# Up product of three groups of eight by seven block products, with weight sums made by accumulating loads

## The chip, the cores and the metric

One core of one Trainium2 chip runs the whole computation as one program. The metric is the device time of one execution in microseconds (us). TensorE (PE) multiplies, VectorE (DVE), ScalarE (ACT) and GpSimd (POOL) do elementwise work, SyncE (SP) starts loads. The engines run side by side; each takes its own instructions in order and waits on semaphores.

## The reference

```python
def sqrelu_mlp(h, w1, w2):                      # w1 (1024, 4096), w2 (4096, 1024)
    u = jax.nn.relu(jnp.einsum('bsd,df->bsf', h, w1))
    return jnp.einsum('bsf,fd->bsd', u * u, w2)

for i in range(2):                              # h is (1, 512, 1024), float32
    hn = rmsnorm(h, norm_mix[i])
    h = h + (conformer_conv(hn, ...) if i == 0 else pool_mixer(hn, ...))
    h = h + sqrelu_mlp(rmsnorm(h, norm_mlp[i]), mlp_w1[i], mlp_w2[i])
return rmsnorm(h, final_norm)
```

The change concerns `sqrelu_mlp`, the dense part of both layers.

## The kernel before, in words

Every float32 operand is split into a high part, rounded to the multiplier's format, and a low part, the rest. A product is three matmuls: high x high, high x low, low x high (`product`, L1449; its matmuls are L1452 to L1454, those of the block products L1715 to L1717). For every weight or activation, ACT writes the high part (a copy) and DVE the low part (a subtraction).

The 4096 hidden features are cut into 8 groups of 512. A group has an up product and a down product. The up product (`mlp_up`, L1683) makes 4 tiles of 128 features x 512 tokens, each from 8 pieces of depth 128: 4 x 8 x 3 = 96 matmuls of 512 columns. For group 1 it is done in two halves of 256 tokens (`mlp_up_first`, L1720). Then ACT takes relu and square. The down product of groups 1 to 7 (`mlp_middle`, L1693) treats the group's product as 2 x 2 blocks and makes it by seven block products instead of eight (Strassen's scheme in Winograd's form): 7 x 12 = 84 matmuls of 512 columns. It needs sums of activation blocks (`a_sum`, DVE, 512 elements per partition) and sums of weight blocks (`b_sum_of`, DVE, 1024 elements). Two of the seven products stay in PSUM banks 4 to 7 over all groups; the other five go through banks 0 to 3, from which DVE adds them to `acc` or `h` (`add`, L1181). Group 8 is done directly (`mlp_up_last`, `mlp_down`).

The order on each engine is written out by hand. PE alternates up and down of a group without a break in the order. On DVE a group is one list: the low parts of the down weights (`b_low`) and of the next group's up weights (`w1_low`), the low parts of the activation blocks (`a_low`), the sums, and the adds. ACT has the matching list of high parts. SP loads the next group's weights whenever their raw copies have been read: up weights 2 MB at once (`load_m1`, L279), down weights in two halves of 1 MB (`load_m2`, L284). POOL has no work in the dense part, apart from clearing `acc`; earlier, in the convolution, it issues seven accumulating transfers within on-chip memory (L417, 1 MB each).

PE waits, for each piece, on semaphores that count finished low parts (`w1_lo_ok`, `w2_lo_ok`, `u_lo_ok`) and finished adds (`m_added`, since the banks are reused). In a block product these are the two lines

```python
pe.wait_ge(u_lo_ok, 7 * w + (LAYER_SPLITS * layer + i + 1))
pe.wait_ge(w2_lo_ok, 7 * w + (LAYER_SPLITS * layer + i + 1))
```

Of the kernel before, what the change touches and what calls it, by code (L numbers as in the profile page):

```python
# [23 lines left out]
P = 128  # L24
# [30 lines left out]
LAYER_ADDS = NQ + 10 * MIDDLE  # L55
LAYER_SPLITS = GF + 7 * MIDDLE
LAYER_SUMS = 4 * MIDDLE
UP_BANK = (2, 3, 0, 1)
# [5 lines left out]
def hybrid_encoder(nc, x, norm_mix, norm_mlp, conv_w1, conv_b1, conv_dw, conv_dwb, conv_ln_g, conv_ln_b,  # L64
                   conv_w2, conv_b2, pool_w, pool_b, pool_scale, mlp_w1, mlp_w2, final_norm, out):
    ctx = ExitStack()
    with ctx:
# [24 lines left out]
        spare = relu[:].rearrange("p a b -> p (a b)")  # L92
        tok = sb("tok", [P, 2, D])
        gain = sb("gain", [P, 2, D])
        ident = sb("ident", [P, P])

        with ExitStack() as share:
            params = share.enter_context(nc.sbuf_tensor("params", [P, NC, NPAR], F32))
        with ExitStack() as share:
            junk = share.enter_context(nc.sbuf_tensor("junk", [P, D], BF16))  # L100
# [3 lines left out]
        bn = sb("bn", [P, NB, 3, 6])  # L104
# [6 lines left out]

# [6 lines left out]
        with ExitStack() as share:  # L118
# [21 lines left out]
        b11, b12 = m2_raw[:, 0:2, 0:512], m2_raw[:, 0:2, 512:1024]  # L140
        b21, b22 = m2_raw[:, 2:4, 0:512], m2_raw[:, 2:4, 512:1024]
        t1, t2, t3, t4 = b_sum[:, 0], b_sum[:, 1], b12, b21
        a_parts = (a11, s3, a12, a22, s1, s2, s4)
        b_parts = (b11, t3, b21, t4, t1, t2, b22)
# [3 lines left out]
        qb_lo = w2_lo[:].rearrange("p (k f d) -> p k f d", k=4, f=2)  # L148
        c2_hi = (w1_hi[:].rearrange("p (c d) -> p c d", c=NC), w2_hi[:].rearrange("p (c d) -> p c d", c=NC))
# [52 lines left out]
        a_sum_ok, b_sum_ok, acc_zero, banks_read = (  # L202
            sem(n) for n in ("a_sum_ok", "b_sum_ok", "acc_zero", "banks_read"))

        w1_hi_ok, w1_lo_ok, w2_hi_ok, w2_lo_ok = (sem(n) for n in ("w1_hi_ok", "w1_lo_ok", "w2_hi_ok", "w2_lo_ok"))
# [55 lines left out]

        block = ctx.enter_context(nc.Block())
# [3 lines left out]
        def _(sp):  # L266
# [21 lines left out]

            def load_groups(layer):

                sp.wait_ge(w1_lo_ok, 4 * GROUPS * layer + 4)
                load_m1(layer, 1)

                def middle(w, more):
                    parts = LAYER_SPLITS * layer
                    sp.wait_ge(w2_lo_ok, 7 * w + (parts + 2))
                    load_m2(layer, w + 1, 0)
                    sp.wait_ge(w2_lo_ok, 7 * w + (parts + 7))
                    load_m2(layer, w + 1, 1)
                    if more:  # L300
                        sp.wait_ge(w1_lo_ok, 4 * w + (4 * GROUPS * layer + 8))
                        load_m1(layer, w + 2)

                with sp.Fori(0, MIDDLE - 1) as w:
                    middle(w, True)
                middle(MIDDLE - 1, False)
                sp.wait_ge(u_lo_ok, LAYER_SPLITS * layer + (LAYER_SPLITS - GF))
# [32 lines left out]
            for k in range(2):  # L340
                load_m2(0, 0, k)
# [6 lines left out]
            sp.dma_start(gain[:, 1, :], row(pool_scale[0])).then_inc(gain_in[1], 16)  # L348
            sp.wait_ge(turned, 4 * GEN_MLP0 + NB)
            sp.dma_start(pw_raw, pool_w[0].rearrange("g (k p) d -> p (g k) d", p=P)).then_inc(pw_in, 16)  # L350
            load_groups(0)
            sp.dma_start(gain[:, 0, :], row(norm_mix[1])).then_inc(gain_in[0], 16)
            sp.wait_ge(w1_lo_ok, 4 * GROUPS)
# [5 lines left out]
            for k in range(2):  # L359
                load_m2(1, 0, k)  # L360
            sp.wait_ge(tok_ok, 4 * GEN_POOL + NB)
            sp.dma_start(gain[:, 0, :], row(norm_mlp[1])).then_inc(gain_in[0], 16)
            load_groups(1)
# [122 lines left out]
        def _(act):  # L486
# [169 lines left out]
            def w1_high(layer, g, j):  # L656
                if j == 0:
                    act.wait_ge(w1_in, 16 * g + (32, 16 * (GROUPS + 2))[layer])
                nc.scalar.copy(m1_hi[:, j], m1_raw[:, j]).then_inc(w1_hi_ok, 1)  # L659
# [1206 lines left out]
```

## Time and profile before

| | |
|---|---|
| median of 3 runs | 886.23 us (885.8 to 886.63) |
| span of the profiled execution | 884.7 us |
| PE busy | 874.4 us, 99% of the span |
| DVE busy | 700.1 us, 79% |
| ACT busy | 464.1 us, 52% |
| POOL busy | 140.0 us, 16% |
| chain that ended last | PE 95%, DVE 2% |

The span is what the profile covers; no time of its own is given for the profiled execution, and the runs' median is 1.5 us over the span. A matmul is pipelined: its row shows 0.39 us, but the next starts 0.23 us later, so the cost of a matmul in a stream is the distance between starts. The same holds in part for DVE and ACT: two independent instructions in a row overlap a little.

### The profile page before, as it was taken

To read this page: it belongs to the slowest core of one execution; us is meant where nothing else is said; L and a number is where in the kernel's file an instruction comes from. 1 tells how busy PE (TensorE), PEld (TensorE's weight loads), DVE (VectorE), ACT (ScalarE), POOL (GpSimd) and SP (SyncE) were. 2 spreads that over 40 slices of the span, in tenths; PEclk is the share of its full clock that TensorE was granted. 3 is DMA by queue.
4 is the path that set the end of the run, shared out by engine and by line. 5 is a ranking of instruction groups with operands and counts; after the bars stand their busy time and mean duration, and the time that the engine had idled before them with its cause. 6 is when DMAs were issued, how large, how long until landed. Compare 5 with 4: busy or idle time off the path is not lost.

```text
span 884.7 us, 11889 instructions
## 1 busy us (share of the span) xinstructions
PE 874.4 (99%) x4383; PEld 740.7 (84%) x4383; DVE 700.1 (79%) x946; ACT 464.1 (52%) x675; POOL 140.0 (16%) x122
## 2 busy tenths in 40 slices
PE   8999999999999999999999999999999999999997
PEld 8888887899888888888888889988888888888886
DVE  6899999768786968776778788897786968776866
ACT  6898976247272544536273544637272544536243
POOL 1699970560000020000000040000000000000000
PEclk9999999999999999999999999999999999999999
DMA  9766732305413142331314222122313142331202
GB/s 302 198 166 150 188 73 98 143 1 191 143 47 143 57 175 77 118 133 57 142 48 167 77 73 90 48 98 94 142 47 142 52 174 77 125 127 64 72 1 95
DMA packets 49255, 97.62 MB, mean 110 GB/s; under 512 B 1562, under 2 KB 18978, under 8 KB 48324
## 3 DMA queue, kind: packets, MB, share of 16 engines
q1 hardware_dynamic: 48068, 89.54, 29.4%
q0 software_dynamic: 1008, 7.34, 4.0%
q8 instruction: 23, 0.38, 0.2%
q10 hardware_dynamic: 144, 0.26, 0.1%
q14 instruction: 12, 0.10, 0.0%
HBM read 87.70 MB, written 2.10 MB: 101 GB/s over the span
## 4 chain that ended last, share of the span: by engine, by line
PE 95%; DVE 2%; DMA 1%; ACT 1%; issue 0%; SPq 0%; DVEq 0%; ACTq 0%
PE ps L1454 19%; PE ps L1452 19%; PE ps L1453 19%; PE ps L1717 10%; PE ps L1715 10%; PE ps L1716 10%; PE ps L1530 3%; PE ps L1471 1%; PE ps L1629 1%; PE ps L1634 1%; PE ps L1630 1%; DMA h<-in_x 1%; DVE tok L894 0%; DVE act_lo L900 0%; DVE tok L928 0%
## 5 line engine op out<-in xcount | busy, mean ns | idle before, releaser
L1452 PE MATMUL ps<-act_hi,w_hi 128*128 128x512 f32 (+1 forms) x688 | 254.9, 370 | 0.0
L1453 PE MATMUL ps<-act_lo,w_hi 128*128 128x512 f32 (+1 forms) x688 | 254.2, 369 | 0.0
L1454 PE MATMUL ps<-act_hi,w_lo 128*128 128x512 f32 (+1 forms) x688 | 254.2, 369 | 0.0
L1715 PE MATMUL ps<-w_hi,u_hi 128*128 128x512 f32 x392 | 152.7, 390 | 0.0
L1717 PE MATMUL ps<-w_hi,u_lo 128*128 128x512 f32 x392 | 152.7, 390 | 0.0
L1716 PE MATMUL ps<-w_lo,u_hi 128*128 128x512 f32 x392 | 152.5, 389 | 0.0
L685 ACT ACTIVATE relu<-ps 128x512 f32<-128x512 f32 x36 | 21.5, 597 | 242.8 <-PE ps L1454 242.8
L1452 PEld LDWEIGHTS ps<-act_hi,w_hi 128*128 128x128 f32 x688 | 129.7, 188 | 21.8
L1454 PEld LDWEIGHTS ps<-act_hi,w_lo 128*128 128x128 f32 x688 | 129.6, 188 | 21.8
L1453 PEld LDWEIGHTS ps<-act_lo,w_hi 128*128 128x128 f32 x688 | 129.7, 188 | 21.7
L1172 DVE TENSOR_TENSOR w_lo<-w_raw,w_hi 128x1024 fp32r<-128x1024 f32 x70 | 85.1, 1220 | 58.0 <-ACT w_hi L706 58.0
L1118 DVE TENSOR_TENSOR w_lo<-w_raw,w_hi 128x1024 fp32r<-128x1024 f32 x64 | 76.9, 1223 | 12.4 <-ACT w_hi L659 12.4
L1717 PEld LDWEIGHTS ps<-w_hi,u_lo 128*128 128x128 f32 x392 | 73.6, 188 | 15.6
L1716 PEld LDWEIGHTS ps<-w_lo,u_hi 128*128 128x128 f32 x392 | 73.6, 188 | 15.4
L1715 PEld LDWEIGHTS ps<-w_hi,u_hi 128*128 128x128 f32 x392 | 73.6, 188 | 15.2
L706 ACT CAST w_hi<-w_raw 128x1024 fp32r<-128x1024 f32 x70 | 73.0, 1046 | 19.6 <-PE ps L1717 13.3
L1183 DVE TENSOR_TENSOR h<-h,ps 128x512 f32<-128x512 f32 x84 | 57.2, 681 | 31.7 <-PE ps L1717 31.7
L991 DVE SCALAR_TENSOR_TENSOR ps<-upad,params,ps 128x512 f32<-128x512 f32 x107 | 71.2, 748 | 0.0
L659 ACT CAST w_hi<-w_raw 128x1024 fp32r<-128x1024 f32 x64 | 66.3, 1044 | 6.6 <-DMA w_raw<-in_mlp_w 6.6
L560 ACT ACTIVATE prod_a<-upad,params 128x512 f32<-128x512 f32 x64 | 40.4, 712 | 2.6 <-DMA prod_a<-prod_a 2.6
L1183 DVE TENSOR_TENSOR acc<-acc,ps 128x512 f32<-128x512 f32 x56 | 37.0, 680 | 3.4 <-PE ps L1717 3.4
L1172 DVE TENSOR_TENSOR w_lo<-b_sum,w_hi 128x1024 fp32r<-128x1024 f32 x28 | 34.1, 1218 | 0.5 <-ACT w_hi L706 0.5
(237 smaller groups left out, 1264.0 us busy)
## 6 DMA issues: line engine op xcount, KB each, us to landing
w_raw<-in_mlp_w SPq DMA_DIRECT2D x32, 1024.0 KB, 5.0
w_raw<-in_mlp_w SPq DMA_DIRECT2D x16, 2048.0 KB, 8.0
w_raw<-in_conv_w SPq DMA_DIRECT2D x16, 512.0 KB, 5.5
prod_a<-prod_a POOLq DMA_DIRECT2D x7, 1024.0 KB, 7.9
w_raw<-in_conv_w SPq DMA_DIRECT2D x2, 2048.0 KB, 11.0
h<-in_x SPq DMA_DIRECT2D x4, 512.0 KB, 5.8
out<-tok SPq DMA_DIRECT2D x7, 256.0 KB, 2.0
gain<-in_norm_mlp SPq DMA_DIRECT2D x2, 512.0 KB
```

Of the source, the lines that this page charges most:

```text
L659: nc.scalar.copy(m1_hi[:, j], m1_raw[:, j]).then_inc(w1_hi_ok, 1)
L706: nc.scalar.copy(qb_hi[:, i % 4], b_parts[i]).then_inc(w2_hi_ok, 1)
L991: step = nc.vector.scalar_tensor_tensor(into, window, weight, sums[n % 2], ALU.mult, ALU.add)
L1118: nc.vector.tensor_tensor(m1_lo[:, j], m1_raw[:, j], m1_hi[:, j].bitcast(F32), ALU.subtract).then_inc(w1_lo_ok, 1)
L1172: nc.vector.tensor_tensor(qb_lo[:, i % 4], b_parts[i], qb_hi[:, i % 4].bitcast(F32), ALU.subtract).then_inc(w2_lo_ok, 1)
L1183: nc.vector.tensor_tensor(at, at, ps[:, k % 4, :], op).then_inc(m_added, 1)
L1452: nc.tensor.matmul(dst, lh, rh, start=(n == 0), stop=False)
L1453: nc.tensor.matmul(dst, lh, rl, start=False, stop=False)
L1454: return nc.tensor.matmul(dst, ll, rh, start=False, stop=(n == count - 1))
L1715: nc.tensor.matmul(dst, lh, rh, start=(f == 0 and (opens or i not in (0, 5))), stop=False)
L1716: nc.tensor.matmul(dst, lh, rl, start=False, stop=False)
L1717: last = nc.tensor.matmul(dst, ll, rh, start=False, stop=(f == 1 and (closes or i not in (0, 5))))
```

## The change

Groups 2 to 7 of a layer go in pairs. In the first of a pair ("plain", groups 2, 4, 6) the up product stays as it was. In the second ("blocks", groups 3, 5, 7) it is made by seven block products too. Written `w` from 0, group 1 is w = 0, and pair v is w = 2v+1 and 2v+2. The parts of the change:

- PE: a block product of the up side is 2 feature tiles x 4 depth pieces x 3 = 24 matmuls of 256 columns; seven of them make 168.
- Activations: four block sums of the activations (z1 to z4) are made once a layer, on DVE in group 1 (`x_block`, `x_step`, eight instructions), and split (`x_high`, `x_low`).
- Results: the seven products are put together by seven DVE instructions (`sum_two` ... `sum_21`) before relu and square, and one ACT copy.
- Weight sums: the up weights of a blocks group come as four loads of 512 KB. Of the sums, two are made by DVE or are plain blocks; the others grow in one buffer (`w_chain`) by accumulating loads that POOL issues (`add_s1`, `add_s2`, `add_s4`), each after its forerunner has been split. The down weights come as four loads of 512 KB as well; two of the four DVE sums per group become accumulating loads (`add_t2`, `add_t4`).
- Down product: the order of the seven products changes (banks 4 to 7 take the first and the fourth), and each pair of adds of 512 elements becomes one of 1024.
- The load of the pool weights in layer 0 moves behind the last blocks group's up product; the POOL descriptor scratch is set to 4096 bytes.

The core of the diff:

```diff
-LAYER_ADDS = NQ + 10 * MIDDLE
+LAYER_ADDS = NQ + 5 * MIDDLE
+W_AT = (1, 3, 4, 2, 5, 7, 6)
+B_AT = (1, 3, 2, 4, 5, 6, 7)
...
+            def w_source(layer, g, upper_f, upper_k):
+            return (mlp_w1[layer].rearrange("(c p) f -> p c f", p=P)
+                    [:, 4 * upper_k:4 * upper_k + 4, bass.ds(g * 512 + 256 * upper_f, 256)])
...
+            def add_w(layer, g, into, upper_f, upper_k, done):
+                nc.gpsimd.dma_start(into, w_source(layer, g, upper_f, upper_k), accum_op=ALU.add).then_inc(done, 16)
+            def add_s2(layer, v):
+                pool.wait_ge(acc_zero, layer + 1)
+                pool.wait_ge(w1_lo_ok, block_part(layer, v) + W_AT[1])
+                add_w(layer, 2 * v + 2, w_chain, 0, 0, w_chain_added)
...
+                with pool.Fori(0, PAIRS) as v:
+                    add_t2(layer, 2 * v + 1)
+                    add_s1(layer, v)
+                    add_t4(layer, 2 * v + 1)
+                    add_s2(layer, v)
+                    add_s4(layer, v)
+                    add_t2(layer, 2 * v + 2)
+                    add_t4(layer, 2 * v + 2)
...
 # ACT, third and fourth up tile of a plain group, and the late parts
+                    up_tile(n + 2, done + 3, banks[2], squared[1][:, 0], lambda: chain_b(3, 1))
+                    up_tile(n + 3, done + 4, banks[3], squared[1][:, 1])
+                    act.wait_ge(usq_ok, n + 4)
+                    sums_high()
...
 # DVE, group 1 ("first") and plain groups
+                    b_low(0)
+                    if kind == "plain":
+                        w1_low(plain_part(layer, v) + 2, 2)
+                    b_sum_three()
+                    b_sum_one()
+                    if kind == "plain":
+                        w1_low(plain_part(layer, v) + 3, 3)
                     b_low(2)
+                    b_low(1)
+                    if kind == "first":
+                        x_block(layer, 1, z1, 1, 1)
+                        x_block(layer, 2, z3, 0, 1)
+                        x_step(layer, 3, z3, z1, z3, ALU.subtract)
+                        x_block(layer, 4, z2, 0, 0)
+                        x_step(layer, 5, z2, z3, z2, ALU.add)
+                        x_step(layer, 6, z1, z1, z2, ALU.subtract)
+                    third_sum(n + 2)
                     a_low(0)
                     a_low(1)
+                    if kind == "plain":
+                        w_low(layer, v, 0)
+                    b_low(3)
+                    first_sum()
+                    second_sum()
+                    a_low(2)
+                    a_low(3)
+                fourth_sum()
+                if kind == "plain":
+                    w_low(layer, v, 3)
+                b_low(4)
+                add(1, 0, acc[:, 1])
+                a_low(4)
+                if kind == "plain":
+                    w_low(layer, v, 1)
+                add(2, 2, acc[:, 0])
+                b_low(5)
                 a_low(5)
                 b_low(6)
                 a_low(6)
+                add(4, 4, h[:, 0:2, 0:512])
+                if kind == "plain":
+                    w_low(layer, v, 2)
+                    w_sum_three()
+                add(5, 6, h[:, 2:4, 0:512])
+                add(6, 8, h[:, 0:2, 512:D])
+                if kind == "first":
+                    x_low(layer, 0)
+                    x_block(layer, 7, z4, 1, 0)
+                    x_step(layer, 8, z4, z4, z2, ALU.subtract)
+                    x_low(layer, 1)
+                    x_low(layer, 2)
+                    x_low(layer, 3)
...
 # PE, up product of a blocks group
+                for i, bank in enumerate((2, 3, 0, 1, 0, 1, 2)):
+                    pe.wait_ge(w1_lo_ok, n + W_AT[i])
+                    if i < 4:
+                        pe.wait_ge(m_added, 5 * w + (LAYER_ADDS * layer - 1 + i // 2))
...
+                    for j in range(2):
+                        for c in range(4):
+                            nc.tensor.matmul(dst, lh, rh[:, c], start=(c == 0), stop=False)
+                            nc.tensor.matmul(dst, lh, rl[:, c], start=False, stop=False)
+                            last = nc.tensor.matmul(dst, ll, rh[:, c], start=False, stop=(c == 3))
```

## Rows read from the trace of the kernel before

**Rows 1.** The page: busy time by engine, and the granted clock in 40 slices.

```profile
PE 874.4 (99%) x4383; PEld 740.7 (84%) x4383; DVE 700.1 (79%) x946; ACT 464.1 (52%) x675; POOL 140.0 (16%) x122
PEclk9999999999999999999999999999999999999999
```

**Rows 2.** Windows (length; PE, PEld, DVE, ACT, POOL busy; clock; DMA; GB/s): group 3, up, down.

```profile
272.86:294.64 21.78, 21.78 (x98) 18.03 (x97) 15.43 (x15) 11.11 (x15) 0.00 (x0) 1.00 0.31 109
294.64:313.70 19.06, 19.06 (x85) 15.76 (x84) 15.06 (x21) 8.04 (x11) 3.95 (x2) 1.00 0.26 98
```

**Rows 3.** Windows, one middle group of 40.80 us.

```profile
336.10:376.90 40.80, 40.80 (x181) 33.73 (x181) 30.49 (x36) 19.09 (x27) 0.00 (x0) 1.00 0.29 103
```

**Rows 4.** Timeline of DVE in a middle group's down product.

```profile
340.41 0.68 DVE L1167 TENSOR_TENSOR u_lo<-relu,u_hi 128x512 fp32r<-128x512 f32 x1
341.01 1.22 DVE L1172 TENSOR_TENSOR w_lo<-b_sum,w_hi 128x1024 fp32r<-128x1024 f32 x1
342.15 0.68 DVE L1183 TENSOR_TENSOR acc<-acc,ps 128x512 f32<-128x512 f32 x1
342.75 0.68 DVE L1176 TENSOR_TENSOR a_diff<-gain,relu 128x512 f32<-128x512 f32 x1
```

**Rows 5.** Timeline of DVE, group 1 of layer 0, up to its first down product.

```profile
200.92 1.22 DVE L1179 TENSOR_TENSOR b_sum<-w_raw 128x1024 f32<-128x1024 f32 x1
202.24 1.23 DVE L1179 TENSOR_TENSOR w_raw<-w_raw 128x1024 f32<-128x1024 f32 x1
204.51 3.49 DVE L1172 TENSOR_TENSOR w_lo<-w_raw,w_hi 128x1024 fp32r<-128x1024 f32 x3
208.66 0.69 DVE L1176 TENSOR_TENSOR a_diff<-relu 128x512 f32<-128x512 f32 x1 [0.65 <-ACT relu L689]
209.31 0.69 DVE L1167 TENSOR_TENSOR u_lo<-relu,u_hi 128x512 fp32r<-128x512 f32 x1
```

**Rows 6.** Timeline of ACT after the first up tile of a group.

```profile
319.36 0.60 ACT L685 ACTIVATE relu<-ps 128x512 f32<-128x512 f32 x1 [14.76 <-PE ps L1454]
319.86 1.04 ACT L706 CAST w_hi<-w_raw 128x1024 fp32r<-128x1024 f32 x1
320.79 0.63 ACT L689 ACTIVATE relu<-relu 128x512 f32<-128x512 f32 x1
```

**Rows 7.** Timeline of PE, matmuls of 256 columns, 188.15 to 190.91 (24 in all).

```profile
188.15 0.28 PE L1452 MATMUL ps<-act_hi,w_hi 128*128 128x256 f32 x1
...
190.91 0.28 PE L1454 MATMUL ps<-act_hi,w_lo 128*128 128x256 f32 x1
```

**Rows 8.** Timeline of PE: the first down matmul of layer 0.

```profile
212.92 0.39 PE L1715 MATMUL ps<-w_hi,u_hi 128*128 128x512 f32 x1
```

**Rows 9.** The line of POOL's accumulating transfers, seven of 1 MB.

```profile
L417 POOL DMA_DIRECT2D prod_a<-prod_a x7: 855/863/1044, 37.7 to 115.9; - x7
DMA to landing us min/median/max: 6.9/7.9/12.3
```

**Rows 10.** DMA view of 115 to 124 us, one such transfer alone.

```profile
q0 software_dynamic: 144, 1.05, 57.7%
prod_a<-prod_a POOLq DMA_DIRECT2D x1, 1024.0 KB, 6.9
```

**Rows 11.** DMA view of 60 to 75 us: packets of two kinds.

```profile
q1 hardware_dynamic: 2735, 1.38, 34.7%
q0 software_dynamic: 144, 1.05, 33.7%
```

**Rows 12.** DMA view of 306 to 325 us: the weight loads of a group.

```profile
w_raw<-in_mlp_w SPq DMA_DIRECT2D x1, 2048.0 KB, 7.9
```

More of the change, by code:

```diff
@@ L294, in middle @@
[L294 to L305, printed above, removed]
@@ new lines, in load_groups @@
+                sp.wait_ge(w1_lo_ok, LAYER_PARTS * layer + GF)
+                load_m1(layer, 1)
+                load_first(0)
+                load_rest(0)
+                with sp.Fori(0, PAIRS - 1) as v:
+                    pair(v)
+                pair(PAIRS - 1, closes=True)
+                if layer == 0:
+                    sp.wait_ge(up_mm, block_part(0, PAIRS - 1) + PARTS)
+                    sp.dma_start(gain[:, 1, :], row(pool_scale[0])).then_inc(gain_in[1], 16)
+                    sp.dma_start(pw_raw, pool_w[0].rearrange("g (k p) d -> p (g k) d", p=P)).then_inc(pw_in, 16)
@@ L830, in _ @@
             act_high(GEN_MLP1, 3)
-            mlp_middle(1, 0, True)
-            with act.Fori(1, MIDDLE) as w:
-                mlp_middle(1, w)
+            mlp_middle(1, 0, "first")
+            with act.Fori(0, PAIRS) as v:
+                mlp_middle(1, v, "plain")
+                mlp_middle(1, v, "blocks")
             mlp_up_last(1)
@@ L1156, in mlp_add, with mlp_middle @@
                 nc.vector.tensor_tensor(at, at, mlp_bank(q), ALU.add).then_inc(m_added, 1)
-            def mlp_middle(layer, w, first=False):
+            def mlp_middle(layer, v, kind):
+                w = {"first": 0, "plain": 2 * v + 1, "blocks": 2 * v + 2}[kind]
                 splits = LAYER_SPLITS * layer
@@ L1206, in mlp_middle, with second_sum, fourth_sum @@
+                def second_sum():
+                    dve.wait_ge(u_lo_ok, 7 * w + (splits + 1))
+                    a_sum(2, s2, s1, a11, ALU.subtract)
+                def fourth_sum():
+                    dve.wait_ge(usq_ok, n + 4)
+                    dve.wait_ge(u_lo_ok, 7 * w + (splits + 2))
+                    a_sum(3, s4, a12, s2, ALU.add)
+                if kind == "blocks":
                     b_low(0)
+                    b_sum_three()
+                    b_sum_one()
+                    w_low(layer, v, 4)
+                    b_low(2)
@@ L1240, in mlp_middle @@
-                dve.wait_ge(a_sum_ok, 4 * w + (sums + 3))
-                dve.wait_ge(u_lo_ok, 7 * w + (splits + 2))
-                a_sum(s4, a12, s2, ALU.subtract)
-                add(2, 0, 2, h_tile(0, 0))
+                    first_sum()
+                    second_sum()
+                    a_low(2)
+                    a_low(3)
+                fourth_sum()
+                if kind == "plain":
+                    w_low(layer, v, 3)
+                b_low(4)
+                add(1, 0, acc[:, 1])
@@ L1244, in mlp_middle @@
+                a_low(4)
+                if kind == "plain":
+                    w_low(layer, v, 1)
+                elif kind == "blocks":
+                    w1_low(plain_part(layer, v + 1), 0)
+                else:
+                    w1_low(plain_part(layer, 0), 0)
+                add(2, 2, acc[:, 0])
+                b_low(5)
                 a_low(5)
-                add(2, 1, 3, h_tile(1, 0))
-                b_low(5)
-                add(3, 0, 4, h_tile(2, 0), ALU.subtract)
                 b_low(6)
@@ L1381, in _ @@
             act_low(GEN_MLP1, 3)
-            mlp_middle(1, 0, True)
-            with dve.Fori(1, MIDDLE) as w:
-                mlp_middle(1, w)
+            mlp_middle(1, 0, "first")
+            with dve.Fori(0, PAIRS) as v:
+                mlp_middle(1, v, "plain")
+                mlp_middle(1, v, "blocks")
             mlp_up_last(1, lambda j: merge(1, j))
```

601 lines of the change are left out of this document (419 added, 182 removed).

## The prediction

> **What bounds the kernel now.** I read the page first: PE is busy for 99% of the span at full granted clock [rows 1], so only fewer or shorter matmuls, or a PE that waits, can move the time. Then windows on one middle group: 96 up matmuls take 21.78 us and 84 down matmuls 19.06 us, 0.227 us each, the group 40.84 us, with no gap [rows 2]. The same group keeps DVE busy for 30.5 us and ACT for 19.1 us [rows 3]. So PE is the bound, and DVE has 10 us to spare in a group; but its list is in fixed order, so the question is whether single results come in time for PE, more than whether the sum fits. Last the timelines, for the distance from start to start: on DVE 0.60 us after an instruction of 512 elements and 1.14 after one of 1024, 1.22 where the next needs its result [rows 4]; up to 1.32 in a dependent pair [rows 5]. On ACT 0.50 and 0.95 [rows 6].
>
> **The matmuls.** A blocks group replaces 96 matmuls of 512 columns (21.78 us) by 168 of 256. In the stream of narrow ones, 24 starts span 2.76 us, 0.120 each [rows 7]. 168 x 0.120 = 20.16 us, so a blocks group saves 1.62 us, and three in each of two layers save 9.7 us. That is all the change can give; the work on other engines gives nothing back while PE is the bound.
>
> Half of 0.227 would be 0.1135, and 16 us; the row says that a narrow matmul costs more than half a wide one. The Trainium skill (TensorE: Matmul & The Clock Gate, Back-to-back issue gap) gives N / 2.4 + 2.5 ns for an isolated stream: 216 ns for 512 columns and 109 for 256, by which the saving would be an estimated 14.5 us. The rows show 227 and 120, both 11 ns over it, and 11 ns on 168 matmuls instead of 96 is what the saving loses.
>
> **Group 1: the activation sums.** Before, DVE begins the group's list at 200.92, the low part that the first block product needs is done at 209.31 + 0.69 = 210.0, and PE begins the down product at 212.92: 2.9 us of slack [rows 5, 8]. The change takes out one of three weight sums ahead of it (-1.14 us net; the ACT handshakes around the two that are left give some of it back, since the high part of b_low(2) can only start when the second sum is done) and puts six sums of 1024 elements in, each waiting for the last: 6 x 1.22 = 7.3 us [rows 4]. The slack of 2.9 becomes a wait of 7.3 - 1.1 - 2.9 = 3.3, and I take 3.4 for the handshake. Nothing covers it: PE has nothing else queued, it stands in the wait for `u_lo_ok`. The bounds: 2.9 (1.14 each) to 3.9 us (1.32 each) [rows 5]. Both layers: 6.8 us.
>
> **The chain of accumulating loads.** All depends on L, the time from POOL's issue to the landing of 512 KB. Row: an accumulating 1 MB alone lands after 6.9 us, median 7.9, 12.3 at worst beside other loads [rows 9, 10]. In the window of 9 us its packets take 57.7%, 5.2 us, so about 1.8 us are fixed. Half the bytes: 1.8 + 2.6 = 4.4 us, the lower end. But those pieces were 8 KB; an up-weight piece is now 1 KB, eight times as many, and comes from HBM. Loads of 512-byte pieces took 34.7% of 15 us x 16 engines for 2735 packets, 0.03 us each [rows 11], so the fixed part of a piece is below 0.03, and 28 more pieces per engine cost at most 0.8 us. POOL's own 0.86 us for writing 128 pieces would be 3.4 for 512 if it grew in proportion: +2.6. Upper end 4.4 + 0.8 + 2.6 = 7.8, and to 9 if other loads are beside it. I take L = 5.5, nearer to the row of the transfer alone.
>
> The Trainium skill (DMA: Bandwidth & Descriptors, Anatomy of one DMA) gives about 2.0 us + bytes / 436e3 for a load issued by POOL: an estimated 3.2 us here, 4.4 for 1 MB. The row of 6.9 for 1 MB speaks against it for accumulating transfers; by it the waits of the next paragraphs would nearly vanish and the time be that of the first rival.
>
> In a plain group, from the start T of the down product: ACT's relu and square of the last tile end at T + 1.4; DVE then has s1, s2, a_low(2), a_low(3), s4 (3.2 us with their waits), w_low(3), b_low(4), add(1) (3 x 1.14), a_low(4) 0.60 and w_low(1) 1.22: T + 9.9. There POOL issues s2. When it has landed, ACT's high part (1.04), w_low(2) (1.14), the sum s3 (1.14) and add(5) (1.22) follow, since add(5) is queued behind them on DVE: T + 9.9 + L + 4.5. PE wants bank 2, which add(5) frees, for the up product of the blocks group at T + 19.06. So PE waits L - 4.65 us: 0.87 at L = 5.5. Before, the adds stood at the end of the list behind nothing that a transfer could hold. The second and third pair of a layer pay this: 1.7 us per layer.
>
> **The first pair is worse.** After its adds of group 1, DVE still has six instructions for the activation blocks, 7.0 us. They move group 2's list: counted from the start of the up product, add(6) ends at 1.3, those six at 8.3, the five before b_low(2) at 14.0, b_low(2) at 15.2 instead of 8.2, and only then may POOL issue t2. ACT waits for t2 between the relu of the third tile and its square, and relu of the fourth tile stands behind. It shares the DMA engines with the 2 MB of the blocks group, issued at the same time and 7.9 us on their way [rows 12], so I give it L + 2.6 = 8.1 us: 15.3 + 8.1 + 0.95 + 0.5 + 0.6 = 25.4, and PE needs that relu at 21.8 + 2.7 = 24.5. Wait 0.9. From there a_low(5) is 11.3 us of DVE list away and PE's fifth block product 4 x 2.72 = 10.9 plus the start of the list, which leaves 1.0, and 0.2 for an add. The s2 chain then starts 0.7 later against PE than in the other pairs: 0.87 + 0.7 = 1.6. Together 3.7 us per layer (0.7 at L = 4.4; 7.8 at L = 7.4).
>
> **Edits that cost nothing.** The 1024-element adds instead of two of 512 (1.14 for 1.20) [rows 4]; the seven sums after the up product of a blocks group: small DVE instructions, 18 per group against 11, in a group with 39.2 us of PE and, by counting its list (19 x 1.14 + 18 x 0.60), 32.5 us of DVE. The copy and sums between block product seven and down product two have 2.7 us of the first down product over them: three dependent steps of 0.68, relu 0.60 included where it counts. If that cover were gone it would cost 1 to 2 us per blocks group. s1, s4, t4 and the sixth down part have 8 us or more from issue to use, so they show from L = 8 on. The moved pool weights have the up product of group 8 over them (21.8 us against 6 for loading and 4.8 for scaling on POOL).
>
> **The sum.** Per layer 3.4 + 3.7 + 1.7 = 8.8 us of waits, less 4.9 saved: +3.9. Two layers: +7.8 us, on a span of 884.7 and 1.5 around it, the median of 886.2: **894.0 us**. Slower.
>
> **Rivals.**
> - *The accumulating loads hide* (the other side: not slower). One mechanism: s2 lands within 4.65 us of its issue, so add(5) is never late. The lower end of 4.4 is for it, the smaller pieces against. (The 3.2 us of the Trainium skill's DMA: Bandwidth & Descriptors would be for it too.) Then a layer waits 3.4 + 0.7 and saves 4.9: 886.2 - 1.6 = 884.6. It decides at about L = 4.7, where waits equal the saving.
> - *They are long.* L = 7.4, as by POOL writing four times the pieces: 3.4 + 7.8 + 2 x 2.7 = 16.6 per layer, less 4.9, twice: +23.4, 909.6. For it, the 12.3 us beside other loads [rows 9]; against it, that s2 runs nearly alone.
> - *Narrow matmuls at half price*, or DVE's list in group 1 less late than counted, with loads hidden: 16.3 or 9.7 saved against 8 or 2 of waits, 878 in both. Against it, the even distance of 0.120 in this very mix of operands [rows 7].
> - *PE's queues don't block as read*, and the change costs nothing net though the loads are as forecast: within 1.5 us of 886.
>
> **Chances.** Forecast (L from 4.9 to 6.6, 888.5 to 902) 0.52; long 0.20; hidden loads 0.14; cheap matmuls or no hold in group 1 0.09; no net effect 0.05. The range 884.4 to 906 leaves out the cheap case and the long tail. Two tenths of a percent, 1.8 us, is what can be told from no change here: faster (below 884.4) 0.11, within 0.15, slower 0.74.
>
> **What would show it.** The first down matmul of each layer's group 1 with an idle of about 3.4 us, released by DVE's low part. Idle of 1 us ahead of the up product of groups 5 and 7, released by an add, and more ahead of group 3. Accumulating loads of 512 KB landing in 5 to 6 us. The narrow matmuls 0.120 apart. I am wrong if PE stays at 99% busy, or if idle PE time lies inside the blocks groups, where I have none.

## The result, and the profile after

The changed kernel takes 927.08 us (median, 925.02 to 928.47); the kernel before, on the same chip, 886.49 (885.8 to 886.89). The ratio is 1.0457, with a 95% interval of 1.0444 to 1.0470: slower by 4.6%. The forecast was 894.0 with a range up to 906. The direction was right; the extra time is five times what I gave it (40.6 us instead of 7.8).

The page of the kernel after, in the parts that answer to [rows 1]:

```profile
span 926.8 us, 13179 instructions
PE 880.6 (95%) x4815; PEld 762.2 (82%) x4815; DVE 751.7 (81%) x938; ACT 498.3 (54%) x707; POOL 197.9 (21%) x168
PE   8999999998988999999898999899899989999997
PEclk9999999999999999999998999999999999999999
q0 software_dynamic: 18128, 31.46, 20.4%
PE 57%; DVE 26%; DMA 8%; issue 5%; ACT 3%; DVEq 0%; SPq 0%; POOLq 0%; ACTq 0%
```

PE went from 99% busy to 95%, and a quarter of the chain that ended last is now DVE's. What PE waited for (engine and line that waits, what released it, us in total, times, longest):

```profile
PE ps L2063 <- DVE h L1492: 17.5, 6, 4.1
PE ps L2097 <- DVE u_lo L1464: 12.9, 5, 3.8
PE ps L2097 <- ACT gain L841: 4.9, 2, 3.4
PE ps L1832 <- POOL ident L501: 1.7, 1, 1.7
```

The fourth line was there before; the other three are new, 35.3 us in thirteen waits. L2063 is the first matmul of a blocks group's up product, which waits for add(5) to free its bank; L2097 is a down matmul behind an activation's low part, or behind ACT's relu of the group's last up tile. Counted as distance from start to start beyond 0.227 or 0.120 us, the same thirteen gaps are 37.5 us.

That explains 37.5 - 9.7 = 27.8 us of the 42.1 by which the span grew (884.7 to 926.8). The rest doesn't show as waiting. PE's timeline behind the first of the gaps, in group 1 of layer 0:

```profile
216.90 0.79 PE L2097 MATMUL ps<-w_hi,u_hi 128*128 128x512 f32 x1 [3.61 <-DVE u_lo L1464]
217.49 0.63 PE L2098 MATMUL ps<-w_lo,u_hi 128*128 128x512 f32 x1
217.92 0.63 PE L2099 MATMUL ps<-w_hi,u_lo 128*128 128x512 f32 x1
...
219.62 0.54 PE L2097 MATMUL ps<-w_hi,u_hi 128*128 128x512 f32 x1
220.01 0.39 PE L2098 MATMUL ps<-w_lo,u_hi 128*128 128x512 f32 x1
```

The starts are 0.43 us apart, not 0.227: half the clock, 1.2 GHz instead of 2.4, for seven matmuls, which cost 220.01 - 216.90 - 7 x 0.227 = 1.5 us more. The windows show it as granted clock (columns as in [rows 2]; the clock stands after the five busy times):

```profile
200.00:210.00 10.00, 10.00 (x85) 10.00 (x85) 8.85 (x8) 5.77 (x8) 1.27 (x1) 1.00 0.66 232
210.00:220.00 10.00, 6.39 (x35) 5.57 (x34) 8.59 (x9) 3.69 (x6) 0.11 (x1) 0.83 0.30 52
490.00:500.00 10.00, 6.19 (x17) 4.61 (x16) 8.43 (x7) 3.51 (x5) 3.80 (x2) 0.66 0.34 115
600.00:610.00 10.00, 10.00 (x33) 7.97 (x34) 7.99 (x10) 8.09 (x12) 1.21 (x1) 0.72 0.45 90
```

In the last of them PE is 100% busy and starts 33 matmuls of 512 columns in 10 us, where 44 would fit. Seven such stretches cost 13.0 us (1.5, 1.6, 1.5, 2.6, 2.8, 1.6, 1.5), longer distances of single matmuls 1.7. Each of the seven follows one of the ten gaps of 2.5 us or more; three of these ten (3.6, 3.0 and 2.9 us) and the three gaps below 2 us are followed by none. So: gaps 37.5, low clock 14.7, narrow matmuls -9.7, together +42.5, against a measured +42.1.

### The profile page after: what moved, and what is told of

Its sections match the earlier page's. It is cut to its first block, busy times and chain, and to the rows that moved or that the text cites. A ratio compares the mean times of both kernels' runs of the same rounds, so it can differ in the third digit from the quotient of the medians.

```text
span 926.8 us, 13179 instructions
## 1 busy us (share of the span) xinstructions
PE 880.6 (95%) x4815; PEld 762.2 (82%) x4815; DVE 751.7 (81%) x938; ACT 498.3 (54%) x707; POOL 197.9 (21%) x168
## 3 DMA queue, kind: packets, MB, share of 16 engines
q0 software_dynamic: 18128, 31.46, 20.4%
## 4 chain that ended last, share of the span: by engine, by line
PE 57%; DVE 26%; DMA 8%; issue 5%; ACT 3%; DVEq 0%; SPq 0%; POOLq 0%; ACTq 0%
PE ps L1799 8%; PE ps L1797 8%; PE ps L1798 8%; DVE ps L1236 7%; PE ps L2097 5%; PE ps L2098 5%; PE ps L2099 5%; PE ps L2063 5%; PE ps L2065 4%; PE ps L2064 4%; DMA w_raw<-in_mlp_w 4%; DMA b_sum<-in_mlp_w 3%; DVE w_lo L1469 2%; DVE w_lo L1390 1%; PE ps L1816 1%
## 5 line engine op out<-in xcount | busy, mean ns | idle before, releaser
L1797 PE MATMUL ps<-act_hi,w_hi 128*128 128x512 f32 (+1 forms) x496 | 180.5, 364 | 0.0
L1799 PE MATMUL ps<-act_hi,w_lo 128*128 128x512 f32 (+1 forms) x496 | 179.5, 362 | 0.0
L1798 PE MATMUL ps<-act_lo,w_hi 128*128 128x512 f32 (+1 forms) x496 | 179.5, 362 | 0.0
L2097 PE MATMUL ps<-w_hi,u_hi 128*128 128x512 f32 x392 | 156.8, 400 | 17.8 <-DVE u_lo L1464 12.9
L1797 PEld LDWEIGHTS ps<-act_hi,w_hi 128*128 128x128 f32 x496 | 93.7, 189 | 14.8 <-issue 0.3
L1799 PEld LDWEIGHTS ps<-act_hi,w_lo 128*128 128x128 f32 x496 | 93.6, 189 | 14.5
L2097 PEld LDWEIGHTS ps<-w_hi,u_hi 128*128 128x128 f32 x392 | 75.3, 192 | 36.7 <-DVE u_lo L1464 12.4
L2099 PEld LDWEIGHTS ps<-w_hi,u_lo 128*128 128x128 f32 x392 | 75.1, 192 | 16.2
L851 ACT CAST w_hi<-b_sum 128x1024 fp32r<-128x1024 f32 x42 | 43.9, 1046 | 69.8 <-DVE b_sum L1479 48.9
L869 ACT CAST w_hi<-w_raw 128x1024 fp32r<-128x1024 f32 x42 | 43.6, 1051 | 61.0 <-DMA w_raw<-in_mlp_w 46.8
L1390 DVE TENSOR_TENSOR w_lo<-w_raw,w_hi 128x1024 fp32r<-128x1024 f32 x42 | 50.8, 1222 | 27.9 <-ACT w_hi L869 27.9
L1469 DVE TENSOR_TENSOR w_lo<-w_raw,w_hi 128x1024 fp32r<-128x1024 f32 x56 | 68.3, 1220 | 0.0
L851 ACT CAST w_hi<-w_raw 128x1024 fp32r<-128x1024 f32 x56 | 58.7, 1048 | 17.6 <-PE ps L2099 17.6
L1492 DVE TENSOR_TENSOR h<-h,ps 128x1024 f32<-128x1024 f32 x42 | 50.7, 1219 | 18.5 <-PE ps L2099 18.3
L2063 PE MATMUL ps<-act_hi,w_hi 128*128 128x256 f32 x144 | 43.8, 304 | 17.5 <-DVE h L1492 17.5
## 6 DMA issues: line engine op xcount, KB each, us to landing
w_raw<-in_conv_w SPq DMA_DIRECT2D x2, 2048.0 KB, 10.7
```

The source lines that it names most:

```text
L851: nc.scalar.copy(qb_hi[:, i % 4], b_parts[i]).then_inc(w2_hi_ok, 1)
L1390: nc.vector.tensor_tensor(wp_lo[:, i % 4], w_parts[i], wp_hi[:, i % 4].bitcast(F32), ALU.subtract).then_inc(w1_lo_ok, 1)
L1469: nc.vector.tensor_tensor(qb_lo[:, i % 4], b_parts[i], qb_hi[:, i % 4].bitcast(F32), ALU.subtract).then_inc(w2_lo_ok, 1)
L1492: nc.vector.tensor_tensor(at, at, ps[:, k % 4:k % 4 + 2, :], ALU.add).then_inc(m_added, 1)
L1797: nc.tensor.matmul(dst, lh, rh, start=(n == 0), stop=False)
L1798: nc.tensor.matmul(dst, lh, rl, start=False, stop=False)
```

## The experiments

"The changed kernel" is the one of 927.08 us. The gaps of each run are counted from the PE timeline of its one profiled execution in the same way. "Slow matmuls" is what the half-clock stretches and the longer distances of single matmuls cost together, 14.7 us in the changed kernel. In the diffs "..." marks lines left out, and the arguments of `x_block` and `x_step` are left out too.

**The adds first.** In plain groups add(5) goes ahead of the wait for the low part of s2's sum:

```diff
+                if kind == "blocks":
+                    w1_low(plain_part(layer, v + 1) + 1, 1)
+                elif kind == "first":
+                    w1_low(plain_part(layer, 0) + 1, 1)
+                add(5, 6, h[:, 2:4, 0:512])
                 if kind == "plain":
                     w_low(layer, v, 2)
                     w_sum_three()
...
-                add(5, 6, h[:, 2:4, 0:512])
                 add(6, 8, h[:, 0:2, 512:D])
```

> In every plain group the add of banks 2 and 3 stands ahead of w_low(2) and w_sum_three on DVE, so it no longer waits for the accumulating load s2. Theory A (PE waits for that add because it is queued behind s2): the six idle stretches ahead of the up product of groups 3, 5 and 7 (4.22, 2.56, 3.04, 2.90, 2.95 and 2.80 us, 18.5 in all) go, and with them the four stretches of half clock behind them (1.60, 1.48, 1.56, 1.48: 6.1 us): 927 - 24.6 = about 902.5 us. Rival B (the load itself is late for PE): the idle time moves to the third up block product, which needs w_low(2), and the time stays above 915 us.

Measured 904.37 us, 1.0207 (1.0182 to 1.0233): 22.7 us less than the changed kernel, though only an add changed places with two instructions. The line "PE <- DVE h" is gone from its waits:

```profile
PE ps L2097 <- DVE u_lo L1464: 11.2, 3, 4.0
PE ps L2097 <- ACT gain L841: 5.4, 2, 3.1
```

The six gaps were 18.5 us; the slow matmuls shrank by 3.5 us (14.7 to 11.2) and the gaps that are left by 1.5, 23.5 in all against 23.4 between the two traced executions. This is close to what theory A said (902.5). It was the place of add(5) in DVE's queue that let a transfer hold PE, and nothing that PE itself needed from s2.

**The same loads without accumulation.** The POOL loads only overwrite; bytes, places and waits stay.

```diff
-, accum_op=ALU.add).then_inc(done, 16)
+).then_inc(done, 16)
```

> POOL's loads of the weight blocks don't accumulate (the weight sums are left out, the block is only overwritten); issue, size and waits are the same. Theory A (an accumulating load is slower than a plain one of the same pieces by the read and add on the chip's side): landing falls from 6.0 and 6.6 us to under 5, and the time to about 915 us. Rival B (what costs is the small pieces and POOL's writing of them): landing stays at 6 us and the time at 927.

Measured 903.12 us, 1.0191 (1.0172 to 1.0210), below both. Issue and landing, first of the changed kernel (instruction's duration in ns min/median/max, then issue to landing in us, for the loads of L581):

```profile
L581 POOL DMA_DIRECT2D w_raw<-in_mlp_w x18: 1264/1296/1316, 257.6 to 835.6; - x18
DMA to landing us min/median/max: 6.0/6.6/11.3
```

and without accumulation, with its queue's row (packets, MB, share of 16 engines):

```profile
q0 software_dynamic: 7632, 31.46, 11.9%
L581 POOL DMA_DIRECT2D w_raw<-in_mlp_w x18: 748/768/777, 258.5 to 812.4; - x18
DMA to landing us min/median/max: 4.1/4.3/8.3
```

The same 31.46 MB go in 7632 packets instead of 18128; POOL writes them in 0.77 us instead of 1.30, and they land 2.3 us sooner. The add gaps, 2.6 to 4.2 us each, fall to 0.58 to 0.84, all gaps together from 37.5 to 18.4 us and the slow matmuls from 14.7 to 8.6: 24 us less, twice the 12 of theory A. The pieces are the same in both, so rival B, small pieces and POOL's writing of them, is out as the main cost. The packets say what accumulation does. Seven 1 MB transfers take 7 x 144 = 1008 of either number [rows 10]. The 46 loads of the change have 6624 left without accumulation, 144 each; with it 17120, which is 18 x (512 + 16) + 28 x (256 + 16): one packet for every contiguous piece, of 1 KB in the 18 up-weight loads and of 2 KB in the 28 down-weight loads, where the plain load makes 144 of any. But the number of packets isn't the whole cost: beyond the plain load, 528 packets cost 2.3 us of landing time (6.6 against 4.3) and 272 cost 2.0 (6.0 against 4.0). What the rest goes into was not separated.

**Without the activation sums.** The eight sums and four splits per layer are left out, on ACT and DVE; the products take plain quarters. The part on PE:

```diff
-                        pe.wait_ge(x_lo_ok, X_PARTS * layer + right[i] + 1)
-                        rh, rl = x_hi[right[i]], x_lo[right[i]]
+                    cs, cols = act_quarter(*(right[i] if i in (0, 3, 5) else (i % 2, i // 4)))
+                    rh, rl = act_hi[:, cs, cols], act_lo[:, cs, cols]
```

> Leaves out the four activation block sums and their split; the blocks products read plain quarters of the activations in their place, so the number and size of matmuls is the same. Theory A (the sums on DVE hold group 1 and delay the list of group 2): the idle of 3.77 and 3.78 us in group 1 goes, with 1.5 and 2.8 us of half clock; group 2 keeps only what the other pairs have, so its three idle stretches of 8.96 and 5.61 us become about 2.8 each; 927 - 11.9 - 9.0 - 1.6 = about 904.5 us. Rival B (group 2 is late because its loads are slow, not because of the list): only the first part goes, 915 us.

Measured 909.31 us, 1.0249 (1.0231 to 1.0268): 17.8 us less. Group 1's gap falls from 3.8 to 1.4 and 0.9 us, and both gaps inside group 2 are gone, but its add gap stays (4.4 and 2.7). The miss of 5 us against theory A's 904.5 is what stays: in layer 0 the sums are not all of the first pair's extra wait (4.4 us against the 2.7 to 2.8 of the other pairs), and in group 1 a wait for ACT's relu takes the place of the sums, behind the split of the chained load:

```profile
PE ps L2074 <- ACT gain L841: 1.9, 2, 1.2
```

**The pool weights later.** The two SP loads go behind the last `load_m2` of the layer.

```diff
-                if layer == 0:
-                    sp.wait_ge(up_mm, block_part(0, PAIRS - 1) + PARTS)
-                    sp.dma_start(gain[:, 1, :], row(pool_scale[0])).then_inc(gain_in[1], 16)
-                    sp.dma_start(pw_raw, pool_w[0].rearrange("g (k p) d -> p (g k) d", p=P)).then_inc(pw_in, 16)
...
                 load_m2(layer, GROUPS - 1, 1)
+                if layer == 0:
+                    sp.wait_ge(up_mm, block_part(0, PAIRS - 1) + PARTS)
+                    sp.dma_start(gain[:, 1, :], row(pool_scale[0])).then_inc(gain_in[1], 16)
+                    sp.dma_start(pw_raw, pool_w[0].rearrange("g (k p) d -> p (g k) d", p=P)).then_inc(pw_in, 16)
```

> The two loads for the pooling layer (0.5 and 1 MB) are issued after the last down weights and not beside the accumulating load t4 of group 7 in layer 0. Theory A (t4, 10.66 us there against 6.0 in the median, is slow because of them, and POOL's multiplications, which start when they land, slow DVE): idle of 3.97 us and 2.6 us of half clock go, 920.5 us. Rival B (t4 is late for another reason): 927 us, and t4 still takes over 9 us.

Measured 919.83 us, 1.0376 (1.0359 to 1.0393), near theory A's 920.5: 7.3 us for a step that I had costed at nothing. In the changed kernel (timelines of POOL, SP, DVE and PE in group 7's down product of layer 0):

```profile
476.94 1.19 POOL L584 DMA_DIRECT2D b_sum<-in_mlp_w  x1 [11.31 <-DVE w_lo L1469]
488.10 5.70 POOL L631 TENSOR_TENSOR tok<-tok,gain 128x1024 f32<-128x1024 f32 x2 [9.98 <-DMA tok<-in_pool_w]
...
477.41 0.43 SPq L409 DMA_DIRECT2D tok<-in_pool_w  x1
...
488.71 2.88 DVE L1469 TENSOR_TENSOR w_lo<-b_sum,w_hi 128x1024 fp32r<-128x1024 f32 x1 [1.85 <-ACT w_hi L851]
491.51 2.84 DVE L1464 TENSOR_TENSOR u_lo<-gain,u_hi 128x512 fp32r<-128x512 f32 x1
494.28 1.21 DVE L1469 TENSOR_TENSOR w_lo<-w_raw,w_hi 128x1024 fp32r<-128x1024 f32 x1
...
494.41 0.80 PE L2097 MATMUL ps<-w_hi,u_hi 128*128 128x512 f32 x1 [3.81 <-DVE u_lo L1464]
```

Two things meet. POOL's chained load t4 and the pool weights are issued 0.5 us apart, and both take some 10.7 us until their user starts. Then POOL scales the pool weights, 2.85 us an instruction, and DVE's two instructions beside it take 2.88 and 2.84 us, where such ones take 1.22 and 0.69. The first of them waits for t4, and the second is what PE waits for. The Trainium skill (SBUF — State Buffer, Who interferes with whom) says that a DVE instruction with two SBUF inputs contends with a GpSimd instruction that reads SBUF; these rows agree, and show that even an instruction of half the length runs for as long as POOL's.

The late load alone would have cost PE next to nothing: by an estimate from these rows, with the usual 1.14 and 0.69 us the second one ends at 490.5, and PE has its matmul queued from 490.4. In the run without accumulation DVE doesn't wait for t4 at all, and the same two instructions beside POOL still take 3.17 and 2.84 us (gap 2.3). And it matters which instructions stand beside POOL. The kernel before had these two multiplications in the dense part as well (it is not so that POOL only cleared `acc` there), beside adds with one input in a PSUM bank, and neither side got slower, POOL at 2.4 us each and DVE at 0.64 (1.28 for two):

```profile
309.49 1.28 DVE L1183 TENSOR_TENSOR acc<-acc,ps 128x512 f32<-128x512 f32 x2
309.75 4.76 POOL L474 TENSOR_TENSOR tok<-tok,gain 128x1024 f32<-128x1024 f32 x2 [117.53 <-DVE w_lo L1118]
```

With the loads later it is so again (POOL 4.79 us for both at 498.60, DVE's adds beside them as fast as ever), and t4 lands after 5.3 us instead of 10.7.

The gap (4.0 us) and its half-clock stretch (2.6) are gone, 6.6 us, and the medians differ by 7.3. That the two agree so well is in part luck. The trace has eight half-clock stretches where the changed kernel's has seven, behind other gaps, and the gaps that both have are 3.5 us shorter, 2.7 of them in the first pair of layer 0 (6.3 us instead of 9.0), which runs ahead of the edit. A single traced execution gives such gaps to 1 to 3 us only.

**Both queue moves.** The adds first and the pool weights later.

> The add first and the pooling loads late; the activation sums stay in group 1. By the two kernels with one of these moves each (904.4 and 919.8 against 927.1): 904.4 - 7.3 = 897.1 us. Left are the two idle stretches of 3.77 us in group 1 with 1.5 to 2.9 us of half clock behind each, and those of group 2's relu, 2.5 to 3.3 us with 1.5. Rival B: the moves don't add up, because one covers part of the other, above 900 us.

Measured 897.82 us, 1.0125 (1.0111 to 1.0140). The two moves add: 22.7 + 7.3 = 30.0, and 29.3 are measured, as forecast (897.1). What is left is group 1 (gaps of 3.8 us) and the ACT relu of group 2 behind t2 (3.5 us), in each layer, and a gap of 1.1 us in group 2 of layer 1.

**Three moves.** The activation sums and splits leave group 1 as well. They are spread over group 2 and the start of group 3 (the last two splits, with `b_low(1)` behind one of them), and the first pair is taken out of the loop on ACT and DVE for it. Whether writing the pair out changes the time by itself was not tried.

```diff
+                early = isinstance(v, int) and v == 0 and kind != "first"
...
                     b_low(1)
-                    if kind == "first":
-                        x_block(1), x_block(2), x_step(3), x_block(4), x_step(5), x_step(6)
+                    if early and kind == "plain":
+                        x_block(1), x_block(2)
                     third_sum(n + 2)
...
                         w_low(layer, v, 0)
+                    if early and kind == "plain":
+                        x_step(3), x_block(4), x_step(5)
                     b_low(3)
+                    if early and kind == "plain":
+                        x_step(6), x_block(7), x_step(8)
...
+                if early and kind == "plain":
+                    x_low(layer, 0)
                 add(5, 6, h[:, 2:4, 0:512])
+                if early and kind == "plain":
+                    x_low(layer, 1)
```

> The add of banks 2 and 3 first, the pooling loads late, and the activation sums moved out of group 1: the eight sums stand in the up product of group 2, where DVE waits for relu and square, the four splits at its end and in group 3 (the first pair is written out of the loop for that). Theory A (every idle stretch comes from the order of the DVE list or from the pooling loads, and the saving of 9.7 us by narrow matmuls is real): idle of 2 to 4 us in all is left, no half clock, 879 us, faster than before the change. Rival B (the accumulating loads hold the list in other places as well): new idle ahead of the third up block product or in the down products, over 886 us.

Measured 885.55 us, 0.9995 (0.9986 to 1.0003): the time of before, not the 879 of the theory. Eight gaps of 0.6 to 1.6 us, 8.1 us in all, and some 2 us of longer distances of single matmuls use up the 9.7. There is no half clock: the windows of these groups show a granted clock of 1.00 (the next expectation calls 2.7 us half-clock stretches; they are single matmuls). All gaps are in groups 1 to 3. Rival B had a part in it, since the longest, 1.56 us in group 1, stands behind the chained load. In the later half of group 2 and the start of group 3 DVE now works without a pause, from 255.2 to 297.4 us. If that is the cause, each us taken out of this stretch comes out of the gaps; the next three runs try it.

**Three sums back into group 1.** The first three sums stand in group 1, behind the second activation split, and one split less in group 3.

```diff
+                    if kind == "first":
+                        x_block(1), x_block(2), x_step(3)
                     b_low(3)
...
-                        x_low(layer, 2)
                         b_low(1)
...
+                if early and kind == "plain":
+                    x_low(layer, 2)
                 add(6, 8, h[:, 0:2, 512:D])
```

> The version with all three moves, with its activation sums placed once more: the first three of the nine steps (3.4 us of VectorE) go into group 1, behind the second activation split, where VectorE of the trace of three moves idles 5.2 us (211.62 to 216.86) for the weight split behind the chained load; the other six stay in group 2, and the third of the four activation splits goes to the end of group 2 instead of into group 3's up product. The theory (a us of VectorE in a stretch where it is saturated is a us of TensorE, the same us in VectorE's idle time is free): the gaps of 1.10, 0.81 and 1.00 us (layer 0) and 1.10, 0.84 and 1.01 us (layer 1) in groups 2 and 3 go, 5.9 us together, the gap of 1.56 and 0.62 us behind the late chained load in group 1 stay, and the half-clock stretches (2.7 us) stay or shrink: 885.6 - 5.9 = 879.7, range 878 to 882.5. The rival (VectorE has no slack left in group 1 either, since TensorE waits there for whatever is put ahead of the fourth weight split): group 1's gap grows by up to 3.4 us per layer with its half-clock stretch, and the time is 885 to 890.

Measured 886.48 us, 1.0001 (0.9992 to 1.0010): a miss, by 6.8 us. Group 1 took the sums for next to nothing (in layer 0 its gap fell from 1.56 to 0.77, in layer 1 it grew from 0.3 to 0.7). But I had emptied 2.9 us of DVE's time at the start of group 2 and put nothing there, so that the later half of the group was as full as before. Of the gaps that were to go, those of group 2 stayed (0.97 and 1.13 us), and the two of group 3, 0.8 and 1.0, became one of 1.88 in each layer. Behind the one in layer 1 the clock fell to half, which cost 1.4 us.

**Sums into idle time.** The fourth and fifth sum go ahead of `third_sum` in group 2, the sixth ahead of `b_low(3)`.

```diff
                     b_low(1)
+                    if early and kind == "plain":
+                        x_block(4), x_step(5)
                     third_sum(n + 2)
```

> The version before it had three activation sums moved into group 1's idle time of VectorE, but left 2.9 us of VectorE idle at the start of group 2 (244.06 to 247.04, waiting for the relu of ScalarE) that the version of three moves had filled with two sums, and so was no faster (gap of 1.88 us behind a late sum in group 3, in both layers). Here the fourth and fifth steps (2.5 us) go into that idle time, and the sixth into the 1.5 us at 252.9 to 254.5; nothing else changes. The theory (a us counts only where VectorE is saturated from there to the next need of TensorE): VectorE enters the second half of group 2 about 3.4 us earlier than with three moves, the gaps of 0.97 and 1.13 us in group 2 and 1.88 us in group 3 of both layers go, with the half-clock stretches behind them (1.6 us in layer 1): 886.5 - 7.5 = 879.0, range 877.5 to 881.5. The rival (what binds in groups 2 and 3 is the landing of the chained loads or another chain, not VectorE's queue): the gaps move by less than 1 us, and the time is 885 to 888.

Measured 884.60 us, 0.9973 (0.9961 to 0.9984), 5.6 us over the forecast. The gaps in group 2 went (0.6 us are left in layer 1), and the half clock (none is left in this trace, in group 1 either, though the next expectation counts on some); those in group 3 stayed, and the gap of group 1 in layer 0 was back at 1.5, with no edit there. The trace says why group 3 gained nothing. DVE in group 2:

```profile
250.63 1.22 DVE L1393 TENSOR_TENSOR x_raw<-x_raw,tok 128x1024 f32<-128x1024 f32 x1
254.94 1.23 DVE L1469 TENSOR_TENSOR w_lo<-b_sum,w_hi 128x1024 fp32r<-128x1024 f32 x1 [3.09 <-ACT w_hi L851]
```

It idles 3.1 us for the split behind t2 and then does the last two sums, which wait for nothing there.

**The last two sums ahead of that wait.**

```diff
+                        x_block(7), x_step(8)
                     b_low(3)
-                    x_block(7), x_step(8)
```

> The version before it left VectorE idle for 3.09 us (251.8 to 254.94, layer 0) and 3.55 us (layer 1) in group 2, waiting for the weight split behind a chained load, and ran the last two activation sums (2.5 us) right behind that wait; the gap of 1.86 and 1.88 us in group 3 behind a late sum stayed. Here these two sums stand ahead of that wait; nothing else changes. The theory: VectorE is 2.5 us earlier from there on, both gaps of 1.9 us go, those of group 1 (1.5 us and its half-clock stretches) stay: 884.6 - 3.7 = 880.9, range 879.5 to 882.5. The rival (the sum in group 3 is late because of another chain, the loads of the blocks behind it): the time stays at 884 to 885.

Measured 882.90 us, 0.9960 (0.9947 to 0.9974). DVE there now:

```profile
249.65 1.22 DVE L1393 TENSOR_TENSOR x_raw<-x_raw,tok 128x1024 f32<-128x1024 f32 x1
250.90 1.23 DVE L1393 TENSOR_TENSOR gain<-act_hi,act_lo 128x1024 f32<-128x1024 f32 x1
252.16 1.23 DVE L1393 TENSOR_TENSOR gain<-gain,tok 128x1024 f32<-128x1024 f32 x1
253.47 1.23 DVE L1469 TENSOR_TENSOR w_lo<-b_sum,w_hi 128x1024 fp32r<-128x1024 f32 x1
256.74 0.69 DVE L1488 TENSOR_TENSOR relu<-relu,gain 128x512 f32<-128x512 f32 x1 [2.05 <-ACT gain L845]
```

It is faster than the kernel before by 0.4%, 3.6 us, the best of all. Its trace has four gaps, 5.2 us in all, some 0.5 us of slow matmuls and no half clock: 5.2 + 0.5 - 9.7 = -4.0, as the spans differ by 3.9 (880.8 against 884.7). So the saving of the narrow matmuls is real. The time is 2.0 us over the forecast of 880.9, since the gaps in group 3 shrank only from 1.9 to 1.6 us, while 1.5 us came from elsewhere. One of two waits:

```profile
290.24 0.39 PE L2075 MATMUL ps<-act_hi,w_hi 128*128 128x256 f32 x1 [1.46 <-DVE relu L1411]
```

The sum that releases it stands behind three low parts in DVE's queue in this first blocks group, and DVE waits for nothing between 257 and 291 us, so the rival, the landing of the loads, doesn't bind there. That its place is what costs the last 3.2 us was not tried.

## Why the prediction was right in sign and wrong in size

The sum was -9.7 for the matmuls and +17.5 for waits. The direction and the places of the waits were right. Three steps failed: the wait for the chained loads came out too short (15 us in all), the move of the pool weights was put at nothing, and no term stood for the clock. Step by step:

- *168 x 0.120 us.* Right. A blocks group's up product of the kernel after runs from 456.72 to 476.83, 20.11 us against the forecast of 20.16:

```profile
456.72 0.35 PE L2063 MATMUL ps<-act_hi,w_hi 128*128 128x256 f32 x1 [2.88 <-DVE h L1492]
...
476.83 0.39 PE L2097 MATMUL ps<-w_hi,u_hi 128*128 128x512 f32 x1
```

- *Group 1: "I take 3.4."* Right place, 3.77 and 3.78 measured, inside the bounds. A step waiting for its result took 1.26 us, not 1.22 (DVE, answering to [rows 5]):

```profile
208.00 2.48 DVE L1394 TENSOR_TENSOR x_raw<-act_hi,act_lo 128x1024 f32<-128x1024 f32 x2
210.52 1.22 DVE L1394 TENSOR_TENSOR x_raw<-x_raw 128x1024 f32<-128x1024 f32 x1
...
215.55 0.69 DVE L1488 TENSOR_TENSOR a_diff<-relu 128x512 f32<-128x512 f32 x1
216.16 0.69 DVE L1464 TENSOR_TENSOR u_lo<-relu,u_hi 128x512 fp32r<-128x512 f32 x1
```

- *"PE waits L - 4.65 us: 0.87 at L = 5.5."* Right mechanism, mis-sized term: 2.6 to 3.0 us, four times, 2.8 on average, where 0.9 was forecast. From group 3 to 5 of layer 0, POOL, ACT, DVE and PE:

```profile
361.42 1.28 POOL L581 DMA_DIRECT2D w_raw<-in_mlp_w  x1 [9.67 <-DVE w_lo L1390]
...
367.49 1.05 ACT L869 CAST w_hi<-w_raw 128x1024 fp32r<-128x1024 f32 x1 [6.94 <-DMA w_raw<-in_mlp_w]
...
359.47 1.22 DVE L1390 TENSOR_TENSOR w_lo<-w_raw,w_hi 128x1024 fp32r<-128x1024 f32 x1
...
368.57 1.23 DVE L1390 TENSOR_TENSOR w_lo<-w_raw,w_hi 128x1024 fp32r<-128x1024 f32 x1 [2.14 <-ACT w_hi L869]
369.71 1.22 DVE L1483 TENSOR_TENSOR w_raw<-w_raw 128x1024 f32<-128x1024 f32 x1
370.85 2.35 DVE L1492 TENSOR_TENSOR h<-h,ps 128x1024 f32<-128x1024 f32 x2
...
372.12 0.39 PE L2063 MATMUL ps<-act_hi,w_hi 128*128 128x256 f32 x1 [2.40 <-DVE h L1492]
```

The low part ends at 360.69 (forecast: 0.3 sooner, counted from the down product's start at 350.49). POOL starts its instruction 0.73 us after that, where I had it at once. Issue to landing is 6.1 us, not 5.5. The four steps behind it and PE's start take 372.12 - 367.49 = 4.63, where I had 4.5. That is 0.3 + 0.7 + 0.6 + 0.1 = 1.7 us, which takes 0.87 to the 2.56 of this pair; the other three waits are 0.2 to 0.5 us longer. L itself came out between the two ends worked out from [rows 9 to 11], 4.4 and 7.8 (the fixed part is 6.9 - 5.2 = 1.7 and not 1.8, which changes nothing). Taking 5.5 as "nearer to the row of the transfer alone" was 0.5 to 1.0 us short (these four loads landed after 6.0 to 6.5), and POOL's 0.7 us between the low part and its issue, in no term, cost as much. In that wait 0.87 was a small rest of two long times, so small errors made it three times as long. That L is long because of the accumulation, and not of the pieces, is shown by the plain loads. The Trainium skill's fit (DMA: Bandwidth & Descriptors, Anatomy of one DMA), 3.2 us for these bytes by an estimate, is below even the plain loads' 4.0 and 4.3.

- *The first pair, 3.7 us per layer.* 9.0 in layer 0 and 5.6 in layer 1. In layer 0 t2 was issued 16.2 us after the start of the up product (237.51), not 15.3, and "I give it L + 2.6 = 8.1" was 10.0: 0.9 + 1.9 us, which takes the wait for relu from 0.9 to 3.6. The s2 load took 7.5 us and ended in an add gap of 4.2. Part of this is of the one execution: in the trace of the pool weights later, the same part of the program had t2 at 9.7, s2 at 6.3 and gaps of 6.3 us. The two gaps in the changed kernel:

```profile
265.83 0.50 PE L2097 MATMUL ps<-w_hi,u_hi 128*128 128x512 f32 x1 [3.44 <-ACT gain L841]
...
288.04 0.46 PE L2063 MATMUL ps<-act_hi,w_hi 128*128 128x256 f32 x1 [4.06 <-DVE h L1492]
```

- *"Edits that cost nothing."* True of the seven sums (no gap inside groups 5 and 7's up product) and false of the pool weights. I asked only whether their own user would be late, and not what they would do to the load beside them on the DMA engines and to DVE. "They show from L = 8 on" held for t4, which landed after 10.7; but what cost the 4.0 us was DVE beside POOL. Moving the loads gained 7.3.

- *The clock was in no term.* In the dense part of the kernel before PE had never idled, so no row showed what a gap of PE costs beyond itself. 14.7 us, as much as all the chained waits together were short of.

Against the forecast of +7.8: group 1 +0.8, first pairs +7.2, other pairs +7.9, pool weights +4.0, clock +14.7, together +34.6; forecast and these make 42.4, measured in the traces 42.1. The rival "they are long" (909.6) comes nearest, but by luck: its L of 7.4 was too long (6.0 to 6.5 for s2), and its +23.4 us lies near the 27.4 that are left without the clock because the long L stood in for POOL's late start and for the pool weights.

## What to carry to other kernels

Where TensorE never idles, price a new wait at more than its length: here a gap of 2.5 to 4.2 us cost on average another 1.3 us at half clock (13.0 over ten), and in ten traces no gap up to 1.6 us cost more than itself and a few tenths, so for the same idle time many short gaps are better than a few long ones. Put no instruction that frees a PSUM bank behind one that waits for a transfer in the same queue; that order alone was worth 22.7 of the 40.6 us. And place added work by an engine's idle stretches, one by one in its timeline, since the same eight sums and four splits a layer, 15 us of DVE, took the kernel from +11 to -4 us against the kernel before by their place (897.82 to 882.90; the pair written out of the loop and one weight split moved came with it). Last, ask of a transfer that you move what its user will run beside.

## What the runs showed of the hardware

- An accumulating load of 512 KB landed after 6.6 us (median, 1 KB pieces) or 6.0 us (2 KB) and took 1.30 or 1.19 us of POOL; without accumulation 4.3 or 4.0 us and 0.77 or 0.72. Beside other loads it took up to 11.3 us.
- With accumulation such a load is one packet per contiguous piece and 16 more (528 or 272), without it 144.
- In POOL's loop its instruction began 0.6 to 0.8 us after the DVE instruction that it waited for had ended (36 times in the changed kernel), outside the loop 0.3 to 0.4 (four times).
- Beside POOL's SBUF to SBUF tensor_tensor DVE's with two SBUF inputs lasted 2.88 instead of 1.22 us, and 2.84 instead of 0.69, and POOL's own 2.85 instead of 2.39. DVE's adds with an input in PSUM kept their 0.64 to 0.69 us beside it.
- Half-clock stretches lasted 3 to 6 us and cost 1.5 to 2.8 us each; in the changed kernel they came with seven of ten idle times of 2.5 us or more of PE. Over the ten traces of kernels with the change: with 31 of 39 idle times from 2.3 to 4.4 us, one of four of 1.9 us, and none of 35 of 0.6 to 1.6 us.
